# Key copies out of PSUM divided between ScalarE and VectorE in the first group of the cache attention

## The reference

```python
def _gathered_attention(q, kg, vg, valid):
    ...
    logits = jnp.einsum('bqngd,bqjnd->bqngj', qg, kg).astype(jnp.float32) * (HEAD_DIM ** -0.5)
    logits = jnp.where(valid[:, :, None, None, :], logits, -jnp.inf)
    p = jax.nn.softmax(logits, axis=-1).astype(vg.dtype)
    o = jnp.einsum('bqngj,bqjnd->bqngd', p, vg)
    return o.reshape(B, Q, N_HEADS * HEAD_DIM)
```

## Time and profile before

| | |
|---|---|
| median of 3 runs | 2517.75 us (2514.52 to 2522.97) |
| profiled execution, time | 2518.05 us |
| its span, first to last instruction | 2516.2 us |
| TensorE busy | 2293.1 us, 91% |
| VectorE busy | 1298.7 us, 52% |
| ScalarE busy | 814.2 us, 32% |
| GpSimd busy | 849.7 us, 34% |
| TensorE's mean granted clock | 0.947 of full |

### The profile page before, as it was taken

How to read it: one execution, slowest core, us unless ns; L and a number is a source line. 1 busy time by engine, 2 the same in 40 slices (tenths; PEclk the granted TensorE clock), 3 DMA queues, 4 the chain that set the end, 5 groups by cost and what they waited for, 6 DMA issues and landing times.

```text
span 2516.2 us, 44394 instructions
## 1 busy us (share of the span) xinstructions
PE 2293.1 (91%) x17087; PEld 2129.0 (85%) x17087; DVE 1298.7 (52%) x2284; ACT 814.2 (32%) x1415; POOL 849.7 (34%) x448
## 2 busy tenths in 40 slices
PE   4988999898879999999999799999988999999996
PEld 4966889897659899999999498888866799999995
DVE  3759666671346722132586686667423665123145
ACT  2234333323331433232242443332344134223233
POOL 2411222224534333333543032222444442333340
PEclk9978999999989999999999699999999899999997
DMA  4321212226752223222333021111566331222330
GB/s 120 127 71 30 61 51 54 56 60 209 254 173 84 84 65 86 84 83 84 112 114 97 22 73 51 51 51 52 161 232 208 112 108 51 84 84 84 86 98 36
DMA packets 331197, 239.26 MB, mean 95 GB/s; under 512 B 10648, under 2 KB 310920, under 8 KB 331064
## 3 DMA queue, kind: packets, MB, share of 16 engines
q1 hardware_dynamic: 304424, 154.69, 22.2%
q0 software_dynamic: 21248, 77.07, 8.9%
q10 hardware_dynamic: 5392, 5.65, 0.7%
HBM read 232.42 MB, written 4.96 MB: 94 GB/s over the span
## 4 chain that ended last, share of the span: by engine, by line
PE 77%; DVE 8%; ACT 5%; issue 4%; DMA 3%; POOL 2%; SPq 0%; ACTq 0%; DVEq 0%; POOLq 0%
PE PS L575 55%; PE PS L556 10%; PE PS L905 2%; PE PS L693 2%; POOL KVB L487 2%; PE PB L919 1%; PE PB L790 1%; PE PB L817 1%; DMA KVB<-in_cache_k_dram,IDXH 1%; ACT KTR L1386 1%; PE PB L969 1%; DVE X L1616 1%; DMA KVB<-in_cache_v_dram,IDXH 1%; PE PB L802 1%; DVE SQ L1603 1%
## 5 line engine op out<-in xcount | busy, mean ns | idle before, releaser
L439 POOL TENSOR_TENSOR WL<-ST,WH 128x1024 fp32r<-128x1024 f32 x290 | 705.0, 2432 | 1439.2 <-ACT WH L1089 1438.6
L1089 ACT CAST WH<-ST 128x1024 fp32r<-128x1024 f32 x290 | 303.5, 1046 | 959.0 <-PE PS L575 795.2
L575 PE MATMUL PS<-AXh,WH 128*128 128x280 f32 x2656 | 589.8, 304 | 14.0 <-POOL WL L439 9.3
L575 PE MATMUL PS<-AXl,WH 128*128 128x280 f32 x2656 | 567.6, 295 | 0.0
L575 PE MATMUL PS<-AXh,WL 128*128 128x280 f32 x2656 | 564.8, 294 | 0.0
L575 PEld LDWEIGHTS PS<-AXh,WH 128*128 128x128 f32 x2656 | 430.1, 192 | 26.9 <-issue 13.1
L575 PEld LDWEIGHTS PS<-AXl,WH 128*128 128x128 f32 x2656 | 431.3, 192 | 0.0
L575 PEld LDWEIGHTS PS<-AXh,WL 128*128 128x128 f32 x2656 | 428.3, 192 | 0.0
L575 PE MATMUL PS<-AHh,WH 128*128 128x280 f32 x1152 | 243.8, 293 | 3.5 <-DVE AHl L2019 3.4
L575 PE MATMUL PS<-AHl,WH 128*128 128x280 f32 x1152 | 244.3, 293 | 0.0
L575 PE MATMUL PS<-AHh,WL 128*128 128x280 f32 x1152 | 242.3, 292 | 0.0
(11 more groups left out here) (283 smaller groups left out, 3320.1 us busy)
## 6 DMA issues: line engine op xcount, KB each, us to landing
ST<-in_w_in_dram SPq DMA_DIRECT2D x114, 512.0 KB, 3.9
ST<-in_w_up_dram SPq DMA_DIRECT2D x64, 512.0 KB, 4.2
ST<-in_w_down_dram SPq DMA_DIRECT2D x64, 512.0 KB, 3.8
ST<-in_w_conv_out_dram SPq DMA_DIRECT2D x16, 512.0 KB, 3.8
ST<-in_w_attn_out_dram SPq DMA_DIRECT2D x16, 512.0 KB, 3.9
ST<-in_w_o_dram SPq DMA_DIRECT2D x16, 512.0 KB, 3.8
NAT<-in_x_prompt_dram SPq DMA_DIRECT2D x4, 512.0 KB, 3.9
o_y_dram<-NAT ACTq DMA_DIRECT2D x4, 512.0 KB, 2.6
```

The lines of the kernel that those rows point to most:

```text
L439: pool.tensor_tensor(WL[slot][:, :, :], ST[s][:, :, :], WH[slot][:, :, :].bitcast(F32), ALU.subtract).then_inc(lo_done[s], 1)
L575: mm = pe.matmul(out[:, h, 0:RH], x[:, k, :], y[:, k, RH * h:RH * h + RH], start=(k == 0 and y is hi and x is WH[slot]), stop=(k == KC - 1 ...
L1089: act.copy(WH[slot][:, :, :], ST[s][:, :, :]).then_inc(hi_done[s], 1)
```

## The change

In group 0 ScalarE copies only the even tiles (a step of `2 - g` in its loop) and counts `kt_ea`; VectorE copies the odd tiles and counts `kt_ed`. In group 1 ScalarE copies all 32, as before. TensorE's waits are rewritten to match: a transpose waits for one of the two semaphores, logits in group 0 for both.

```diff
+        def k_copied(l, g, t):
+            if g == 1:
+                return kt_ea, l * 48 + 16 + t + 1
+            return (kt_ea, l * 48 + t // 2 + 1) if t % 2 == 0 else (kt_ed, l * 16 + t // 2 + 1)
+        def k_before(t):
+            return t - 3 if t < 17 else t - 2
...
-                            pe.wait_ge(kt_e, l * 64 + 32 * g + (t - 2 if t < 16 else 14 if t == 16 else 16 if t == 17 else t - 1))
+                            pe.wait_ge(*k_copied(l, g, k_before(t)))
...
-                        pe.wait_ge(kt_e, l * 64 + 32 * g + 4 * q + 4)
+                        if g == 0:
+                            pe.wait_ge(*k_copied(l, g, 4 * q + 2))
+                        pe.wait_ge(*k_copied(l, g, 4 * q + 3))
...
-                        for t in range(t0, t1):
+                        for t in range(t0, t1, 2 - g):
...
-                            act.copy(KTR[t % 4][:, :], k_bank(t)).then_inc(kt_e, 1)
+                            act.copy(KTR[t % 4][:, :], k_bank(t)).then_inc(kt_ea, 1)
...
                 gb(0)
                 for g in range(2):
                     for c in range(4):
+                        for t in range(8 * c + 3 if c > 0 else 1, min(8 * c + 10, 32), 2):
+                            if g == 0:
+                                dve.wait_ge(kt_t, l * 64 + t + 1)
+                                if t >= 4:
+                                    dve.wait_ge(kt_mm, l * 16 + t // 4)
+                                apart(dve, started)
+                                dve.tensor_copy(KTR[t % 4][:, :], k_bank(t)).then_inc(kt_ed, 1)
                         dve.wait_ge(ls_mm, l * 10 + 5 * g + c + 1)
                         dve.reduce_max(st[:, c:c + 1], PB[:, c, :], AX_X)
```

More of the change, by code:

```diff
@@ L323, in trunk_program @@
         kv_in = [[sem(f"kv_in{s}{b4}") for b4 in range(4)] for s in range(2)]
-        kt_t, kt_e, kt_mm = sem("kt_t"), sem("kt_e"), sem("kt_mm")
+        kt_t, kt_ea, kt_ed, kt_mm = sem("kt_t"), sem("kt_ea"), sem("kt_ed"), sem("kt_mm")
         gb_mul, o_split, conv_done = sem("gb_mul"), sem("o_split"), sem("conv_done")
```

## The result

The changed kernel takes 2532.43 us (median of 7 runs, 2526.69 to 2539.59), the kernel before 2519.46 us in the same sets of runs (7, 2514.52 to 2522.97). The ratio is **1.0057, 95% interval 1.0036 to 1.0077**: slower by 0.6%, some 14 us. The profiled execution took 2529.08 us, its span is 2527.3 us. Executions of one and the same kernel spread over 8 and 13 us in these runs, so that one pair of profiles is no measure of the total. Inside the group of the change, though, the profiles agree with one another within a few tenths of a microsecond, and most of what follows is read there.

The account below looks back on a forecast made before the run. The prediction took TensorE, with 77% of the chain, as the bound; 5.9 + 5.4 us at the first logits and 0.2 us behind them made 11.5 us on 2518.05, 0.3 above the median: 2529 us, range 2522 to 2533.

Parts of the forecast that it names:

- Tile 4 late by 5.22 and 4.30 us: At the group's start, tile 4 waits for tile 1's copy behind VectorE's gate multiply: 5.22 us in layer 0, 4.30 in layer 1.
- The clock, 4.3 to 4.9 us at 1.2 GHz behind the wait: After tile 4's wait, TensorE's work runs at the lower clock, 1.2 GHz, for 4.3 to 4.9 us.
- The rival of a clock that comes back at once: Behind tile 4's wait TensorE runs at full rate: 7.3 us late in all, 2525 us; chance 0.17.
- First logits late by 5.9 and 5.4 us: The group's first logits end 5.9 us late in layer 0 and 5.4 us late in layer 1.
- The rest of the group, +0.1 us a layer: Behind the first logits, odd copies cost at most 0.4 us and gain at most 0.35: +0.1 us a layer.
- The multiply held by GpSimd until its subtraction ends: VectorE's gate multiply at the group's start takes 3.28 us, not 0.74, held until GpSimd's WL subtraction is done.
- The rival in which it takes 0.74 us: VectorE's gate multiply isn't held: 4.5 to 5 us, 2522.5 us; chance 0.14, shared with a delay partly swallowed later.
- Nothing swallows the delay: Behind the group, later gathers and waits slide with TensorE, so the whole 11.5 us reaches the kernel's end.
- ScalarE the brake: In the group, odd copies off ScalarE's queue free the even ones too, saving 7.9 us of waits: 2510 us; chance 0.04.
- the forecast's own upper case, 2532: Upper end for the whole kernel with multiply held and clock low, 2527.5 to 2532 us; chance 0.65.

Follow-up runs that it names:

- e5: The changed kernel with tiles 1 and 3 of the first group back on ScalarE and no semaphore step ahead of VectorE's key copies: 2516.25 us, ratio 1.0003.
- e3: The changed kernel with GpSimd's WL subtraction for gate chunk 2 put behind the gathers of key chunk 2, some 10 us later: 2520.62 us, ratio 1.0022.
- e2: The changed kernel with only tiles 1 and 3 of the first group copied by VectorE, all others by ScalarE: 2528.50 us, ratio 1.0050.
- e8: The changed kernel with VectorE's gate chunk put behind its copies of tiles 1 and 3: 2519.21 us, ratio 1.0016.

## Why the prediction was right or wrong

The direction, the place and the mechanism were right; the forecast was 11.5 us, and 12.7 us were measured in the group of the profiled execution. Step by step:

- *Tile 4 late by 5.22 and 4.30 us.* Measured from tile 0 on: 5.10 and 4.18.
- *The clock, 4.3 to 4.9 us at 1.2 GHz behind the wait.* Measured 5.3 and 5.0, both above the range that I took from two rows. The rival of a clock that comes back at once is out.
- *First logits late by 5.9 and 5.4 us.* Measured 6.02 and 5.44. That they came so near is in part luck: tile 4 was 0.12 us less late than forecast, and the low clock lasted longer.
- *The rest of the group, +0.1 us a layer.* **This term was mis-sized: it is +0.63 in each layer, 1.26 us in the sum and not 0.2.** I had counted the longer copy, 0.10 us each for tiles 21, 25 and 29 and the last logits, against a gain of up to 0.35 us at tile 17. What I had not counted is that VectorE's copy begins 0.18 us behind the transposes where ScalarE's begins 0.04 us behind. So these four lost 0.14 to 0.2 us each, and tile 17, from which I had taken a gain, lost 0.2 too (ScalarE's copy of tile 15 had begun 0.14 us behind its transposes, hardly queued at all), while tiles 8, 9 and 16 gained 0.05 to 0.1. e5 shows where it comes from: the semaphore step ahead of the copy. Without it the rest is +0.05 and -0.06 us.
- *The multiply held by GpSimd until its subtraction ends.* Right: 3.25 and 3.24 us again, and 0.74 in e3. It ends 0.6 us behind the subtraction (592.33 against 591.72 in layer 0). The rival in which it takes 0.74 us falls; its price was too low as well, since e3, where the multiply does take 0.74 us, has 7.0 us in the two groups and not 4.5 to 5. The Trainium skill ("SBUF — State Buffer", section "Who interferes with whom") says of such a pair that the two exclude one another and that the one issued first goes through. The first agrees: 3.25 us beside the subtraction, 0.74 us in e3. As to the second, the multiply's row starts 0.3 us first in the earlier trace rows and is the one held; so the starts of the rows don't tell here which one goes through, and which was issued first, no run shows.
- *Nothing swallows the delay.* e2, whose group is 11.5 us longer, is 1.0050 times the time, 12.6 us. In all nine kernels of the table the two groups' sum lies inside the interval of the ratio.
- *ScalarE the brake.* Out: its waits stayed at 3.6 and 3.8 us, and e5, with 14 of the 32 copies off ScalarE and no stall, gains nothing.

The median of the changed kernel, 2532.4, lies in the range. By the ratio and the median of before in the same runs it is 1.0057 x 2519.46 = 2533.8, just past the upper end of 2533. That end was the forecast's own upper case, 2532, and 1 us for the spread of runs; the rest's missing 1.1 us and a spread of 13 us among executions had no room in it. Some 1.7 us of the way from 2529 to 2533.8 are none of the change's: the kernel before took 2519.46 us in these runs, and the forecast started from 2517.75. Between the 12.7 us in the profiled group and the ratio's 14.4 there remain another 1.7 us that no run places; the interval, 9 to 19 us, doesn't need them. (The two profiled executions lie 11.0 us apart, less than their groups' 12.7: the rest of the kernel differs by a few us from one execution to the next.)

## What to carry to other kernels

Before work is handed to an engine because it has idle time, look at where in its program the work lands and at what that engine does in those microseconds: a mean of 52% busy said nothing about the 7 us in which VectorE was taken, and two copies of 0.7 us a layer queued behind them made nearly all of a 12.7 us loss. Of a wait on the bounding engine ask which copy is waited for: nine of ten waits were for tiles that stayed where they were, so a second engine had little to give. Where the bounding engine waits for something that will come anyway, give it independent work to do there; that alone made the kernel before 0.17% faster (0.05 to 0.28%), and in the group's first part it kept the clock up as well.

## What the runs showed of the hardware that I had not expected

With a semaphore increment as an instruction of its own between the waits and VectorE's copy, the copy starts 0.14 us later (0.18 against 0.04 us behind the transposes, changed kernel and e5). The other was read from two pairs of rows before, and the runs bear it out: VectorE's multiply of two SBUF operands, recorded as starting 0.3 us ahead of a GpSimd subtraction, lasted until 0.6 us behind the end of that, 3.24 to 3.29 us in place of 0.74, in the group's start; in e3, 13 us apart, and in e8, behind the subtraction, it took 0.74. It holds of all multiplies of this line in the ten traces: the 56 that overlap a subtraction end 0.61 us behind it, whichever row starts first, and the other 104 take 0.74 us. A multiply of the kernel before whose row starts behind the subtraction's:

```profile
634.25 1.54 DVE L1917 TENSOR_TENSOR BB<-BB,GE 128x560 f32<-128x560 f32 x1
...
632.79 2.40 POOL L439 TENSOR_TENSOR WL<-ST,WH 128x1024 fp32r<-128x1024 f32 x1
```
